# A two-layer hybrid decoder trunk on one core: joined stick-breaking sums, a divided first split, and attention work in another order

## What is computed

```python
def hybrid_mixer(h, positions, w_in, ...):
    u = h @ w_in
    a_out = stick_breaking_attention(sb[:, :, 0], sb[:, :, 1], sb[:, :, 2])   # 4 heads x 64
    b_out = conformer_conv(...)     # GLU, causal depthwise conv w=31, LayerNorm, silu, pointwise
    c_out = dilated_mixture(q, k, dl[:, :, 2])                                # 8 heads x 64, "local"
    return jnp.concatenate([a_out, b_out, c_out], axis=-1) @ w_out

# stick breaking, one head
z = einsum('qc,kc->qk', q, k) * scale
log_keep = where(before, log_sigmoid(-z), 0)
between = cumsum(log_keep, axis=keys, reverse=True) - log_keep
a = where(before, exp(log_sigmoid(z) + between), 0)
out = a @ v
```

## Time and profile before

| | |
|---|---|
| runs of before | 811.47, 814.45 and 2205.48 us, median 814.45 |
| the profiled execution | 811.18 us; its span 809.2 us, 2.0 us lie around it |
| mean granted TensorE clock | 0.999 of full speed |
| DVE, ACT, POOL busy | 652.2, 521.2, 30.5 us |
| DMA | 145.70 MB, 180 GB/s over the span |

### The profile page before, as it was taken

The page is one execution under the profiler, slowest core; times in us unless marked ns, Lnnn a source line. Parts: engine busy times, 40 slices in busy tenths (PEclk is TensorE's granted clock), DMA queues, the critical chain, the costliest instruction groups (busy, mean ns, idle before and its releaser), DMA issues.

```text
span 809.2 us, 12136 instructions
## 1 busy us (share of the span) xinstructions
PE 802.0 (99%) x4608; PEld 696.6 (86%) x4608; DVE 652.2 (81%) x1166; ACT 521.2 (64%) x834; POOL 30.5 (4%) x54
## 2 busy tenths in 40 slices
PE   9999999999999999999999999999999999999997
PEld 7988888889888888888889889888998888888885
DVE  6899996778777999987387999858788489999753
ACT  7847866568556867765365487656866577776441
POOL 1200000100010000000010000001001000000000
PEclk9999999999999999999999999999999999999999
DMA  8755346482574555657566444447545545655651
GB/s 320 270 179 164 127 134 200 135 280 73 189 236 133 163 190 196 206 179 223 173 229 226 142 131 140 148 151 237 180 146 175 175 131 182 208 182 183 234 183 52
DMA packets 40601, 145.70 MB, mean 180 GB/s; under 512 B 4616, under 2 KB 4768, under 8 KB 40544
## 3 DMA queue, kind: packets, MB, share of 16 engines
q1 hardware_dynamic: 38448, 138.30, 52.2%
q0 software_dynamic: 1936, 6.55, 2.4%
q10 hardware_dynamic: 160, 0.09, 0.0%
HBM read 143.87 MB, written 1.05 MB: 179 GB/s over the span
## 4 chain that ended last, share of the span: by engine, by line
PE 98%; issue 1%; DMA 1%; ACT 0%; DVE 0%; SPq 0%; DVEq 0%; POOLq 0%; POOL 0%; ACTq 0%
PE acc L1807 8%; PE acc L1751 5%; PE acc L1753 5%; PE acc L1752 5%; PE psCD L1807 5%; PE acc L1817 4%; PE acc L1768 4%; PE psAB L1807 4%; PE acc L1872 4%; PE acc L1870 4%; PE acc L1871 4%; PE acc L1769 4%; PE acc L1770 4%; PE psAB L1753 3%; PE psAB L1751 3%; PE psAB L1752 3%
## 5 line engine op out<-in xcount | busy, mean ns | idle before, releaser
L1053 DVE TENSOR_TENSOR wlo<-raw,whi 128x1024 fp32r<-128x1024 f32 x240 | 287.7, 1221 | 68.2 <-ACT whi L604 67.1
L604 ACT ACTIVATE whi<-raw 128x1024 fp32r<-128x1024 f32 x240 | 250.1, 1059 | 115.5 <-PE acc L1753 38.6
L1807 PE MATMUL acc<-xT,whi 128*128 128x512 f32 x288 | 89.0, 390 | 0.0
L1807 PEld LDWEIGHTS acc<-xT,whi 128*128 128x128 f32 x288 | 54.1, 188 | 11.8
L1630 DVE SCALAR_TENSOR_TENSOR KT<-V,par,KT 128x255 f32<-128x255 f32 (+1 forms) x144 | 60.0, 480 | 2.1 <-ACT KT L991 1.5
L1817 PE MATMUL acc<-xT,wlo 128*128 128x256 f32 x288 | 58.0, 283 | 0.0
L1341 DVE SCALAR_TENSOR_TENSOR arena<-arena,par 128x256 f32<-128x256 f32 x120 | 50.3, 482 | 0.8 <-ACT arena L820 0.8
L1768 PE MATMUL acc<-xT,whi 128*128 128x256 f32 x176 | 50.6, 288 | 0.0
L1807 PE MATMUL psCD<-xT,whi 128*128 128x512 f32 x160 | 50.0, 394 | 0.0
L1769 PE MATMUL acc<-xT,whi 128*128 128x256 f32 x176 | 49.8, 283 | 0.0
L1770 PE MATMUL acc<-xT,wlo 128*128 128x256 f32 x176 | 49.7, 283 | 0.0
(11 more groups left out here) (369 smaller groups left out, 2060.9 us busy)
## 6 DMA issues: line engine op xcount, KB each, us to landing
raw<-stream_dram SPq DMA_DIRECT2D x256, 512.0 KB, 4.2
gpost<-gain_dram POOLq DMA_DIRECT2D x6, 512.0 KB, 5.7
gpre<-gain_dram POOLq DMA_DIRECT2D x5, 512.0 KB, 6.4
h<-x_dram SPq DMA_DIRECT2D x4, 256.0 KB, 5.9
memn<-mem_dram SPq DMA_DIRECT2D x2, 512.0 KB, 9.2
out_dram<-h SPq DMA_DIRECT2D x4, 256.0 KB, 2.0
cst<-const_dram SPq DMA_DIRECT2D x1, 896.0 KB, 7.6
pww<-pw_dram POOLq DMA_DIRECT2D x2, 256.0 KB, 6.3
```

The costliest lines, as they stand in the source:

```text
L604: act.activation(home(g)[0], raw[:, s * GW:(s + 1) * GW], ACT.Copy).then_inc(w_hi.sem, 1)
L1053: dve.tensor_tensor(lo, raw[:, cols], hi.bitcast(F32), ALU.subtract).then_inc(w_lo.sem, 1)
L1807: e = pe.matmul(up_halves(j, c), whi[:, cols], both, start=k == 0, stop=k == KC - 1)
```

## The change

1. `sb_between` on PE: the two heads of a pair are taken by one product each. The sums of both heads for the queries and keys of the first block (2 x 256 columns) lie in bank `psAB[0]`, those of the second block (2 x 128) in `psAB[1]`. Six products per call instead of twelve. DVE's addition of these sums becomes two instructions.
2. At the start the high part of weight group 0 is made half on DVE and half on ACT, PE's first product waits for the first half alone, the idle products are 8 and 2 instead of 7 and 3, and PE's first passes and flips stand in another order. DVE makes the low part of group 0 ahead of the last two input blocks.
3. `angles_rest` goes one weight group ahead on DVE.
4. The fourth local values (`dl_values(3)`) are written to `psCD[0]`, a bank of the flips, and stand on PE right ahead of `sb_scores(1)`, behind all four key groups instead of behind the first. `mixed_hi(7)` and `mixed_lo(4)` follow them.
5. `sb_between(0)` stands behind three key groups instead of two; `sb_scores(1)` behind the fourth instead of ahead of it; `sb_between(1)` goes from ahead of the convolution's transposes to behind them and behind one more weight group.
6. The slices of taps 23 to 25 on DVE are cut otherwise.

```diff
--- before.py
+++ after.py
@@ -277,6 +277,8 @@
+        early_sums = psAB[0].rearrange("p (h n) -> p h n", h=2)
+        late_sums = psAB[1][:, 0:2 * P].rearrange("p (h n) -> p h n", h=2)
         score_banks = lambda c: psCD if c == 1 else psAB
...
@@ -636,7 +643,8 @@
             first_input_hi(0, 0, 2)
-            split_group(0, 0)
+            act.wait_ge(raw_in[0].sem, raw_in[0].at(0, 1))
+            act.activation(whi[:, NT:GW], raw[:, NT:GW], ACT.Copy).then_inc(w_hi.sem, 1)
             first_input_hi(1, 0)
             split_group(0, 1)
...
@@ -870,10 +878,10 @@
                 split(G_WK1 + AHEAD)
-                mixed_hi(7, o_done, 4, attended)
                 split(G_WK1 + 2 + AHEAD)
                 sb_weights(0)
                 split(G_WK1 + 3 + AHEAD)
+                mixed_hi(7, o_done, 4, psCD[0][:, 0:SEQ])
                 softplus_pair(1)
...
@@ -1130,13 +1138,17 @@
+            def first_weights_hi():
+                dve.wait_ge(raw_in[0].sem, raw_in[0].at(0, 1))
+                dve.tensor_copy(whi[:, 0:NT], raw[:, 0:NT]).then_inc(w0_hi_first.sem, 1)
+
...
@@ -1147,9 +1159,12 @@
             dve.wait_ge(gain0_cols.sem, 1)
+            first_weights_hi()
+            first_input_lo(0, 0, 0, 2)
+            dve.wait_ge(w0_hi_first.sem, 1)
+            split_group(0, 0)
             first_input_rest()
-            first_input_lo(0, 0)
-            split_group(0, 0)
+            first_input_lo(0, 0, 2, 4)
             first_input_lo(1, 0)
             split_group(0, 1)
...
@@ -1373,7 +1388,8 @@
-                    dve.tensor_tensor(view(tt), psA[:, :, 0:AW], view(zs), ALU.add).then_inc(t_ready.sem, 1)
+                    dve.tensor_tensor(view(tt)[:, :, 0:SEQ], early_sums, view(zs)[:, :, 0:SEQ], ALU.add)
+                    dve.tensor_tensor(view(tt)[:, :, SEQ:AW], late_sums, view(zs)[:, :, SEQ:AW], ALU.add).then_inc(t_ready.sem, 1)
...
@@ -1406,10 +1422,11 @@
                     dve.wait_ge(mem_cols_in.sem, 1)
+                    split(g_cv + PER_TILE)
+                    angles_rest()
                     split(g_cv + PER_TILE + 1)
                     dve.wait_ge(root_spread.sem, 1)
                     dve.tensor_copy(root_row, psAB[1][:, 0:SEQ]).then_inc(root_row_in.sem, 1)
-                    angles_rest()
                     memory_lo(0, 0)
...
@@ -1485,13 +1502,13 @@
                 split(G_WK1 + AHEAD)
-                mixed_lo(4, 7, attended)
                 split(G_WK1 + 1 + AHEAD)
+                conv_taps(23, 24)
                 sb_between(0)
-                conv_taps(23, 25)
+                conv_taps(24, 26)
                 split(G_WK1 + 2 + AHEAD)
-                conv_taps(25, 26)
                 sb_masked(1)
+                mixed_lo(4, 7, psCD[0][:, 0:SEQ])
                 split(G_WK1 + 3 + AHEAD)
...
@@ -1725,13 +1744,12 @@
-            idle_products(7)
+            idle_products(8)
...
             first_input(0, 0)
-            idle_products(3)
-            first_input(1, 0)
+            idle_products(2)
...
@@ -1929,7 +1947,7 @@
-                        o, v0 = accs[1][1][r * HD:(r + 1) * HD, :], (2 * c + r) * HD
+                        o, v0 = (psCD[0] if c == 3 else accs[1][1])[r * HD:(r + 1) * HD, :], (2 * c + r) * HD
...
@@ -1947,11 +1965,10 @@
-                        for r in range(2):
-                            k = keep[:, r * AW:(r + 1) * AW]
-                            pe.matmul(psAB[r][:, 0:SEQ], tri, k[:, 0:SEQ], start=first, stop=False)
-                            pe.matmul(psAB[r][:, P:SEQ], ones, k[:, SEQ:AW], start=False, stop=False)
-                            e = pe.matmul(psAB[r][:, SEQ:AW], tri, k[:, SEQ:AW], start=False, stop=not first)
+                        k = keep[:, :].rearrange("p (h n) -> p h n", h=2)
+                        pe.matmul(early_sums, tri, k[:, :, 0:SEQ], start=first, stop=False)
+                        pe.matmul(early_sums[:, :, P:SEQ], ones, k[:, :, SEQ:AW], start=False, stop=not first)
+                        e = pe.matmul(late_sums, tri, k[:, :, SEQ:AW], start=first, stop=not first)
                     e.then_inc(b_done.sem, 1)
...
@@ -1993,13 +2018,14 @@
                     first_pass(both_hi, 0, 0)
+                    first_input(1, 0)
                     first_pass(low_x, 0, 0)
+                    first_pass(low_w, 0, 0)
                     first_pass(both_hi, 0, 1)
                     first_input(0, 1)
-                    first_pass(low_w, 0, 0)
-                    first_input(1, 1)
                     first_pass(low_w, 0, 1)
                     first_pass(both_hi, 1, 0)
+                    first_input(1, 1)
                     first_pass(both_hi, 1, 1)
...
@@ -2086,29 +2112,28 @@
-                transposed_product(G_WK1, 1, M, acc[0])
-                pe.wait_ge(mix_lo.sem, mix_lo.at(l, 3))
-                dl_values(3)
-                transposed_product(G_WK1 + 1, 1, M, acc[0], k0=2)
+                transposed_product(G_WK1, 3, M, acc[0])
                 pe.wait_ge(signs_in.sem, signs_in.at(l, 1))
                 sb_between(0)
-                transposed_product(G_WK1 + 2, 1, M, acc[0], k0=4)
+                transposed_product(G_WK1 + 3, 1, M, acc[0], k0=6)
+                dl_values(3)
                 pe.wait_ge(t_ready.sem, t_ready.at(l, 1))
                 sb_scores(1)
-                transposed_product(G_WK1 + 3, 1, M, acc[0], k0=6)
                 pe.wait_ge(sbv_in.sem, sbv_in.at(l, 1))
-                pe.wait_ge(mix_lo.sem, mix_lo.at(l, 4))
+                pe.wait_ge(mix_lo.sem, mix_lo.at(l, 3))
                 product(G_WV0, 2, M, acc[1])
                 pe.wait_ge(KT_in.sem, KT_in.at(l, 4))
                 sb_values(0, accs[0][0])
-                sb_between(1)
+                pe.wait_ge(mix_lo.sem, mix_lo.at(l, 4))
                 for t in range(TOK):
                     for c in range(2):
                         pe.wait_ge(conv_done.sem, conv_done.at(l, c + 1))
...
-                product(G_WV0 + 2, 2, M, acc[1], k0=4)
+                product(G_WV0 + 2, 1, M, acc[1], k0=4)
+                sb_between(1)
+                product(G_WV0 + 3, 1, M, acc[1], k0=6)
                 sb_values(1, psAB[1])
```

More of the change, by code:

```diff
@@ L1988, in first_pass @@
                             k = g * UNITS + u
+                            if not t:
+                                if k == 0 and hi_w and hi_x:
+                                    pe.wait_ge(w0_hi_first.sem, 1)
+                                else:
+                                    pe.wait_ge((w_hi if hi_w else w_lo).sem, g + 1)
                             e = pe.matmul(acc[0][t], xT[:, 2 * k * SEQ + a0:2 * k * SEQ + a0 + P],
```

22 lines of the change are left out of this document (16 added, 6 removed).

## The result

The changed kernel takes 816.12 us (median of 13 runs, 814.01 to 818.12); the kernel before, run on the same chip, takes 811.57 us. The ratio is 1.0053, with a 95% interval of 1.0044 to 1.0061. So it is slower by 4.6 us, 0.5%: less than the 2% that counts here as a difference, but clearly not zero. The time lies in the forecast range, 1.7 us above the forecast value.

The account below looks back on a forecast made before the run. PE, busy 99% of the span, was taken to bound the kernel; layer 0's +1.75 and layer 1's +1.5 us, joined sums and start included, add 3.25 to the profiled 811.18, giving 814.4 us, range 811.0 to 817.5.

Parts of the forecast that it names:

- PE waits for the last tap: At the convolution's transposes PE arrives before DVE's last tap ends and waits 2.3 us in layer 0, 2.1 in layer 1.
- The sums queued behind it, and the LayerNorm's wait: Behind the transposes, 0.95 us of sums still to come, then PE waits 0.3 for the LayerNorm; layers +1.75 and +1.5 us.
- The joined sums: Each call of sums on PE takes 0.94 us instead of 1.31; 0.37 saved per call, 1.5 us over four calls.
- The start: First groups end 0.5 us earlier, but PE then waits at layer 0's memory keys, so 0.1 us is kept.
- The third key group: In layer 0, PE arrives before this group's split is ready and waits 0.2 us.
- The clock behind the waits: Whether PE's clock falls behind its two pauses of over 2 us; raised only as a rival, 3.35 us if so.
- Rival D: Slower clock behind both waits, half of 3.35 us lost twice, 817.8 us; chance 0.05.
- The range: Whole-kernel time from 811.0 to 817.5 us, including 1.5 us of scatter on top; A and D stay outside.
- the likeliest case: PE waits for the last tap and again for the LayerNorm: 814.4 us, own range 813.3 to 816; chance 0.6.
- The reference: Forecast built on the profiled execution of 811.18 us; median shown 814.45, so noise called as large as the effect.

Follow-up runs that it names:

- experiment 5: Changed kernel with the second call of sums put back ahead of the convolution's transposes: 811.93 us, ratio 1.0010.
- experiment 8: Changed kernel with DVE's list alone altered, the two instructions serving the second sums moved behind the last tap: 812.75 us, ratio 1.0016.
- experiment 1: Kernel before with the joined sums alone, everything else in the old order: 810.80 us, ratio 0.9997.
- experiment 2: Kernel before with the changed start alone (split first group, input order, angles_rest earlier): 810.66 us, ratio 0.9994.
- experiment 4: Kernel before with the new order of the attention alone, sums not joined, old start: 817.13 us, ratio 1.0069.
- experiment 7: Changed kernel with seven unused products ahead of the transposes in one layer only: layer 0 filled 814.45 us, layer 1 filled 816.00 us.

## Why the prediction was right or wrong, point by point

- **PE waits for the last tap: right, a little smaller.** I had 2.3 us in layer 0 and 2.1 in layer 1; it is 1.80 and 1.62. PE arrives at 118.99 - 1.80 = 117.19 (I said 117.34), the last tap ends at 119.24 (I said 119.6), since the second scores and with them `sb_masked(1)` come at 110.73 instead of 111.1. Experiments 5 and 8 show that this wait, and the DVE list behind it, carry the loss.
- **The sums queued behind it, and the LayerNorm's wait: right.** 0.26 us at the back transposes in each layer, 0.3 forecast. Layer 0 costs 3.3 us, of which 1.7 are the clock, so 1.6 against 1.75; layer 1 costs 1.9 against 1.5. Without the clock the terms and their sum hold: 2.7 us in the medians and 4.9 - 1.7 = 3.2 in the two traces, 3.25 forecast.
- **The joined sums: right in size, 0.94 us a call.** Not foreseen is that the first call of each layer is worth nothing in the old order (experiment 1, by its trace).
- **The start: wrong in its mechanism, small in size.** I took one execution's chain at the memory keys for a fixed one. It is fixed only where the DMA is late (experiment 2).
- **The third key group: right.** 0.25 us in each layer, 0.2 forecast.
- **The clock behind the waits: this is the step that failed.** The sum had no term for it, that is 0; the runs show 1.7 us for one stretch in the trace and 1.9 between the groups of runs, in nine of 13 executions. Rival D had the mechanism, the place and the lower level, and a chance of 0.05. It happened once in seven of 13 runs and twice in two. I gave it little because no pause over 0.4 us stood in the trace of before, which said nothing on what a pause of 2 us does; that should have been a case of even chance, with one stretch (816.1) as well as two (817.8). Each stretch costs what D said, 1.7 us, but the way to that figure was in part luck: D took the length from the seven idle products of the start, 3.35 us, and nothing in that trace tied the length of a stretch behind a pause to them. Their distance looks like the lower level, while the granted clock of that window (0 to 4.3 us, kernel before) reads 1.00; no run settles which of the two holds there.
- **The range: wide enough by luck.** 814.4 with 1.5 us of scatter on top is 815.9, and the measured 816.12 lies above that and above the 816 of the likeliest case's own range. 817.5 comes only from adding the scatter to the 816, which already lay 1.6 above the sum, and the text gives no reason for those.
- **The reference: wrong.** The forecast of 3.25 us on a profile of 811.18 stood beside a median of 814.45 from three runs with 3 us between its two undisturbed ones. I wrote that noise is as large as the effect; over the later 71 runs it is not: 64 of them lie between 810.5 and 812 us. The forecast value of 814.4 thus equalled the shown median by accident, and read against that it says "no change", where the text's own sum said slower by 3 us. The profile's own time was the better reference: 3.25 us slower by it, where 4.6 were measured.

## What to carry to other kernels

When the bounding engine's list is reordered, the engine that serves it must be reordered with it: ask of each instruction ahead of the one waited for whether its own consumer has moved back, and put that work behind, or into the idle time. Rearranging DVE's list around the last tap turned a loss of 4.6 us into a gain of 1.5, of which 0.8 was to be had without the new order; whether DVE's new list would have helped the old order too was not run. And price a pause of the matmul engine of nearly 2 us with a possible slow stretch behind it, not only with its length.

## What the runs showed of the hardware that I had not expected

- PE's granted clock fell to the lower level behind a pause of 1.80 us, to judge by the granted clocks in nine of 13 executions of the changed kernel (two of them fell twice) and in three of five with only that pause. Each stretch profiled lasted about 3.4 us (experiments 4 and 7 and the changed kernel) and began 0.4 to 0.8 us behind the end of the pause, within the transposes or just behind them. Pauses of 0.94 us (experiment 8) and of 1.24 and 1.28 at the memory keys (experiments 5 and 4) had none behind them in their profiles, nor had 1.62 and 1.67 (experiment 4) in layer 1. In the ten executions with the pause in layer 0 filled by products that compute nothing, no granted clock was under 0.998.
- The first product of the memory keys scatters with the landing of a DMA: from 33.71 to 35.60 us over three profiles with the old start, from 33.03 to 34.38 over ten with the new one. That is more than most parts of this change are worth. A comparison of traces is better made from a place behind it.
- Of before, one run at 814.34 us had a clock of 0.998, and one of the start alone at 814.20 had 0.997; neither was profiled, and I have no explanation for them.
